# Mamba-2 scan outputs: running sums spread by one product of ones with rows at their own partitions, and a new order of VectorE's boundary work

## The chip, the cores and the metric

One core of one Trainium2 chip runs the whole program in one launch. The metric is the device time in microseconds (us) of an execution; the median of three runs before the change is 5008.08 us.

## The reference

The model is a two-layer backbone over 512 latent tokens and 256 context tokens of width 1024. Each layer has a token mixer (a pooling branch beside a bidirectional Mamba-2 scan) and a product-key expert retrieval. The change lies in the scan's outputs alone. There, tokens are cut into chunks ("tiles" below) of 128, and for each chunk, direction and head:

```python
a_cum = jnp.cumsum(dtc * a, axis=2)                     # running sums in a chunk of 128 tokens
seg = a_cum[:, :, :, None] - a_cum[:, :, None, :]
decay = jnp.exp(jnp.where(lower, seg, -jnp.inf))
cb = jnp.einsum("bclgn,bcsgn->bclsg", cc, bc)
wgt = cb[..., None] * decay * dtc[:, :, None]
y = jnp.einsum("bclsgr,bcsgrp->bclgrp", wgt, xc)        # inside the chunk
y = y + jnp.einsum("bclgn,bcgrpn->bclgrp", cc, h_in) * jnp.exp(a_cum)[..., None]   # from the state
```

Then `d_skip * x` is added to y and the sum is multiplied by `silu(z)`, with a mean square over each of four groups of channels. There are 16 heads in 4 groups of 4, and two directions.

## The kernel before, in words

`stage_outputs` computes this. It runs three times: once for the context of layer 0 (2 tiles), once for the latents of layer 0 and once for those of layer 1 (4 tiles each). Each call is a block of its own: all engines meet before it and after it. No DMA is issued inside it.

A tile (t) has 8 **units**: two directions d times four groups g, called u0 to u7 below (u0 to u3 are d = 0). For each unit:

- GpSimd (POOL) copies the 4 heads' step decays, each repeated along 128 columns, into one of four buffers `dtab` (L855).
- TensorE (PE) multiplies those with a triangle of ones, one 128x128 product for each head (L890): this gives the running sum of every token spread over all partitions, in one of three PSUM banks (`SUMS`). The signal is `acum_ready`.
- ScalarE (ACT) takes the difference to the token's own running sum with four Relu (L929, one for each head) and one Exp (L933) into one of four buffers `m_buf`.
- VectorE (DVE) multiplies with the masked C·B product `cbm` (L966). The signal is `m_ready`.
- PE multiplies the result with dt·x (L872, "intra") and adds it up in the two Y banks. It does so with a lag of two units (`LAG = 2`): in its slot of unit n, PE runs the L890 products of unit n and then the L872 products of unit n-2.

Work that comes once or twice in a tile (**boundary work**):

- PE: C·B for the tile (L883) ahead of u0's products; the product with the incoming state (L902, `inter`), once for each direction, in the slots of u2 and u6, both into the same two banks `INT`, after DVE has read the one before (`inter_read`).
- DVE: two masks of C·B (L958) at u0; `add_y(t-1)` (L945) before u1's product, which reads the Y banks of the tile before and so lets PE start the L872 of the new tile (`y_read`, waited for at u0's L872); `gate(t-1)` (L951) and the skip term (L973) after u1's; the read of `INT` (L978) and its sum (L982) after u3's and u7's.
- ACT: four squares of the tile before (L914) after u3.
- POOL: dt·x of the next tile (L847, two products over 1024 columns) behind the `dtab` copy of u4; it waits for `y_ready` of the tile before.

Every engine goes through its list in program order, and all waits are on semaphores. The order is written by hand.

Of the kernel before, what the change touches and what calls it, by code (L numbers as in the profile page):

```python
# [29 lines left out]
ALU = mybir.AluOpType  # L30
# [4 lines left out]
P = 128  # L35
# [6 lines left out]
HEADS, HEAD_DIM, GROUPS = 16, 64, 4  # L42
HPG = HEADS // GROUPS
# [59 lines left out]
def setup(nc, ctx, io):  # L103
    k = Bag()
# [116 lines left out]
     k.dots, k.lhs_ready, k.slot_free, k.acc_ready, k.acc_read, k.copy_proj, k.copy_ready) = k.sig.values()  # L221
    k.stored = Signal(k, "stored")
    k.decay_ready = Signal(k, "decay_ready")
    for name in ("turn", "h", "proj", "evac", "pad", "conv", "out"):
        k.pre[name] = Signal(k, "pre_" + name)
    k.pre_kept = [Signal(k, f"pre_kept{i}") for i in range(4)]
# [19 lines left out]
def bc(ap, shape):  # L246

    return ap.unsqueeze(2).to_broadcast(shape)
# [565 lines left out]
def stage_outputs(k, stream):  # L814

    nc = k.nc
    T = SEQ if stream == 0 else CTX_LEN
    NT = T // P
# [1 line left out]
    v = mixer_views(k)  # L820
    s = v.scr
    cbm = s[:, 0:1024].rearrange("p (d c) -> p d c", d=2)
    dtab = s[:, 1024:3072].rearrange("p (a h c) -> p a h c", a=4, h=HPG)
    m_buf = s[:, 3072:5120].rearrange("p (a h c) -> p a h c", a=4, h=HPG)
    xd = k.arena[:, A_HT:A_HT + 4 * D].rearrange("p (a d c) -> p a d c", a=2, d=2)
    ysum = s[:, 5120:5120 + D]
# [12 lines left out]
    with nc.Block() as block:  # L839
        @block.gpsimd  # L840
        def _(pool):
            def scale_x(t):

                if t >= 2:
                    pool.wait_ge(k.y_ready.sem, k.y_ready.at(t - 1))
                for dd in range(2):
                    pool.tensor_tensor(heads(xd[:, t % 2, dd]), heads(v.xtok[:, t]),  # L847
                                       bc(v.dt[:, t, dd * 16:dd * 16 + 16], [P, HEADS, HEAD_DIM]), ALU.mult) \
                        .then_inc(k.xd_ready.sem, 1)

            for n, (t, d, g) in enumerate(units):
                if n >= 4:
                    pool.wait_ge(k.acum_ready.sem, k.acum_ready.at(n - 3))
                h0 = d * 16 + g * HPG
                pool.tensor_copy(dtab[:, n % 4], bc(v.dta[:, t, h0:h0 + HPG], [P, HPG, P])) \  # L855
                    .then_inc(k.dtab_ready.sem, 1)
                if n == 0:
                    scale_x(0)
                if g == 0 and d == 1 and t + 1 < NT:
                    scale_x(t + 1)  # L860

        @block.tensor
        def _(pe):
            def intra(n):
                t, d, g = units[n]
                pe.wait_ge(k.m_ready.sem, k.m_ready.at(n + 1))
                pe.wait_ge(k.xd_ready.sem, k.xd_ready.at(2 * t + 2))
                if d == 0 and g == 0 and t >= 1:
                    pe.wait_ge(k.y_read.sem, k.y_read.at(t))
                for h in range(HPG):  # L870
                    hh = g * HPG + h
                    last = nc.tensor.matmul(k.ps[:, Y + g // 2, (hh % 8) * HEAD_DIM:(hh % 8 + 1) * HEAD_DIM],  # L872
                                            m_buf[:, n % 4, h], xd[:, t % 2, d, hh * HEAD_DIM:(hh + 1) * HEAD_DIM],
                                            start=(d == 0 and hh % 8 == 0), stop=(d == 1 and hh % 8 == 7),
                                            skip_group_check=True)
                last.then_inc(k.y_ready.sem if g == GROUPS - 1 and d == 1 else k.group_summed.sem, 1)

            for n, (t, d, g) in enumerate(units):
                if d == 0 and g == 0:
                    if t >= 1:  # L880
                        pe.wait_ge(k.cb_masked.sem, k.cb_masked.at(t))
                    for gg in range(GROUPS):
                        last = nc.tensor.matmul(k.ps[:, CB, gg * P:(gg + 1) * P], v.BT[:, gg, t * P:(t + 1) * P],  # L883
                                                v.CT[:, gg, t * P:(t + 1) * P], start=True, stop=True)
                    last.then_inc(k.cb_ready.sem, 1)
                pe.wait_ge(k.dtab_ready.sem, k.dtab_ready.at(n + 1))
                if n >= 3:
                    pe.wait_ge(k.seg_ready.sem, k.seg_ready.at(n - 2))
                for h in range(HPG):
                    last = nc.tensor.matmul(k.ps[:, SUMS[n % 3], h * P:(h + 1) * P], dtab[:, n % 4, h], k.tri[:, d],  # L890
                                            start=True, stop=True)
                last.then_inc(k.acum_ready.sem, 1)
                if n >= LAG:
                    intra(n - LAG)
                if g == 2 and (t, d) in inters:
                    i = inters.index((t, d))
                    if i >= 1:
                        pe.wait_ge(k.inter_read.sem, k.inter_read.at(i))
                    o = order(d, t)
                    h_in = k.hfin[:, d] if o == 0 else v.hin[:, d, o - 1]  # L900
                    for gg in range(GROUPS):
                        last = nc.tensor.matmul(k.ps[:, INT + gg // 2, (gg % 2) * GW:(gg % 2 + 1) * GW],  # L902
                                                v.CT[:, gg, t * P:(t + 1) * P], h_in[:, gg * GW:(gg + 1) * GW],
                                                start=True, stop=True)
                    last.then_inc(k.inter_ready.sem, 1)
            for n in range(len(units) - LAG, len(units)):
                intra(n)

        @block.scalar
        def _(act):  # L910
            def squares(t):
                act.wait_ge(k.gated.sem, k.gated.at(t + 1))
                for g in range(GROUPS):
                    nc.scalar.activation(sq, v.zs[:, t, g * GW:(g + 1) * GW], ACT.Square,  # L914
                                         accum_out=ss[:, t, g:g + 1])
                    act.drain()

            for n, (t, d, g) in enumerate(units):
                act.wait_ge(k.acum_ready.sem, k.acum_ready.at(n + 1))
                if n >= 4:  # L920
                    tt, dd, gg = units[n - 4]
                    if (dd, gg) == (1, GROUPS - 1):
                        act.wait_ge(k.y_ready.sem, k.y_ready.at(tt + 1))
                    else:
                        act.wait_ge(k.group_summed.sem, k.group_summed.at(n - 3 - tt))
                for h in range(HPG):
                    col = d * 16 + g * HPG + h

                    last = nc.scalar.activation(m_buf[:, n % 4, h], k.ps[:, SUMS[n % 3], h * P:(h + 1) * P], ACT.Relu,  # L929
                                                bias=v.cum[:, t, col:col + 1], scale=-1.0)  # L930
                last.then_inc(k.seg_ready.sem, 1)
                act.drain()
                nc.scalar.activation(m_buf[:, n % 4], m_buf[:, n % 4], ACT.Exp, scale=-1.0) \  # L933
                    .then_inc(k.decay_ready.sem, 1)
                if (d, g) == (0, 3) and t >= 1:
                    squares(t - 1)
            squares(NT - 1)

# [1 line left out]
        def _(dve):  # L940
            def add_y(t):
# [3 lines left out]
                nc.vector.tensor_tensor(ysum, ysum, k.ps[:, Y:Y + 2].rearrange("p a b -> p (a b)"), ALU.add) \  # L945
                    .then_inc(k.y_read.sem, 1)

            def gate(t):

                dve.drain()  # L950
                nc.vector.tensor_tensor(v.zs[:, t], v.zs[:, t], ysum, ALU.mult).then_inc(k.gated.sem, 1)  # L951

            for n, (t, d, g) in enumerate(units):
                if d == 0 and g == 0:
                    dve.wait_ge(k.cb_ready.sem, k.cb_ready.at(t + 1))
                    cb = k.ps[:, CB].rearrange("p (g c) -> p g c", g=GROUPS)
                    for dd in range(2):
                        last = nc.vector.tensor_tensor(cbm[:, dd].rearrange("p (g c) -> p g c", g=GROUPS), cb,  # L958
# [1 line left out]
                                                       ALU.mult)  # L960
                    last.then_inc(k.cb_masked.sem, 1)
                    dve.drain()
                if g == LAG - 1 and d == 0 and t >= 1:
# [5 lines left out]
                if g == LAG - 1 and d == 0:  # L969
                    if t >= 1:  # L970
                        gate(t - 1)
                        dve.drain()
                    nc.vector.tensor_tensor(heads(ysum), heads(v.xtok[:, t]),  # L973
                                            bc(v.hrow[:, HR_SKIP:HR_SKIP + 16], [P, HEADS, HEAD_DIM]), ALU.mult)
                if g == 3 and (t, d) in inters:
                    i = inters.index((t, d))
                    dve.wait_ge(k.inter_ready.sem, k.inter_ready.at(i + 1))
                    nc.vector.tensor_tensor(heads(ytmp), heads(k.ps[:, INT:INT + 2].rearrange("p a b -> p (a b)")),  # L978
                                            bc(v.eac[:, t, d * 16:d * 16 + 16], [P, HEADS, HEAD_DIM]), ALU.mult) \
                        .then_inc(k.inter_read.sem, 1)  # L980
                    dve.drain()
                    nc.vector.tensor_tensor(ysum, ysum, ytmp, ALU.add)  # L982
            add_y(NT - 1)
            gate(NT - 1)
    n = len(units)
# [2 lines left out]
    for x in (k.y_ready, k.y_read, k.gated, k.cb_ready, k.cb_masked):  # L988
        x.advance(NT)
    k.group_summed.advance(n - NT)  # L990
    k.xd_ready.advance(2 * NT)
    for x in (k.inter_ready, k.inter_read):
        x.advance(len(inters))
# [1491 lines left out]
```

## Time and profile before

| what | us |
|---|---|
| runs, median of 3 | 5008.08 (5007.76 to 5017.28) |
| the profiled execution, its own time | 5002.69 |
| its span, first to last instruction | 5000.9 |
| mean granted clock of PE | 0.844 |
| scan outputs, context of layer 0 | 227.8 to 284.0: 56.2 |
| scan outputs, latents of layer 0 | 1396.9 to 1508.7: 111.8 |
| scan outputs, latents of layer 1 | 3276.1 to 3386.2: 110.1 |

The three stages make 278.1 us, 5.6% of the span. The times of the stages are the windows between the first instruction of a stage and the first of the next one. Inside them a tile is read best off ACT: each unit starts with a group of four L929, so the starts of those groups are the beats of the stage, and an idle time printed behind one tells what ACT waited for.

### The profile page before, as it was taken

What the parts mean: (1) busy time and instruction counts of PE and PEld (TensorE: products, weight loads), DVE (VectorE), ACT (ScalarE), POOL (GpSimd) and SP (SyncE); (2) the same over time, 40 slices, a digit from 0 to 9 for tenths busy, and PEclk for the clock granted to TensorE, in tenths of its full rate; (3) what the DMA queues carried; (4) which work ended last, traced back from release to release, by engine and by line L of the source; (5) the groups of instructions that cost most, each with busy time, mean ns of one, the idle gap of its engine ahead of it and who ended that gap; (6) DMA issues with size and microseconds to landing.
All of it is one profiled execution on the core that took longest, in us unless ns stands there. A gap on an engine that the chain in (4) does not pass through costs nothing. (4 is left out here: it accounts for less than half of the span.)

```text
span 5000.9 us, 49209 instructions
## 1 busy us (share of the span) xinstructions
PE 3547.0 (71%) x15992; PEld 1834.1 (37%) x15992; DVE 3231.2 (65%) x6604; ACT 1513.1 (30%) x3714; POOL 2222.5 (44%) x1683
## 2 busy tenths in 40 slices
PE   7888888997578987555555557979988555555555
PEld 5677424332277434111111115877843111111111
DVE  5255687664465567676776766466457777777775
ACT  2352344343142224322222223243222222222221
POOL 3253444443033354555555552333335555555553
PEclk8889999999788998777777778889999777777777
DMA  5436999998603799999999992102279999999998
GB/s 181 177 106 226 376 422 400 419 426 368 259 1 114 278 421 397 413 415 422 403 425 412 414 421 81 68 1 93 77 273 405 423 414 420 419 416 420 414 415 369
DMA packets 251729, 1575.63 MB, mean 315 GB/s; under 512 B 42560, under 2 KB 49216, under 8 KB 65472
## 3 DMA queue, kind: packets, MB, share of 16 engines
q0 software_dynamic: 184320, 1342.26, 64.8%
q1 hardware_dynamic: 67152, 230.23, 12.5%
q8 instruction: 127, 2.08, 0.2%
q14 instruction: 130, 1.06, 0.1%
HBM read 1554.88 MB, written 17.50 MB: 314 GB/s over the span
## 5 line engine op out<-in xcount | busy, mean ns | idle before, releaser
L2349 PE MATMUL banks<-arena 128*64 128x512 f32 x5120 | 1591.6, 759 | 1107.8 <-ACT arena L2177 1107.1
L1964 POOL DMA_INDIRECT arena<-in_experts,arena x1280 | 1504.7, 1176 | 1635.1 <-PE banks L2349 1375.2
L2050 DVE CUSTOM_DVE_ANT_0 arena<-arena,token_copies 128x1024 f32<-128x1024 f32 x1280 | 1636.1, 1297 | 674.1 <-DMA arena<-in_experts,arena 611.6
L2349 PEld LDWEIGHTS banks<-arena 128*64 128x64 f32 x5120 | 385.5, 166 | 2150.6 <-ACT arena L2177 1526.0
L2170 ACT ACTIVATE arena<-arena 128x2 f32<-128x2 f32 x640 | 131.2, 205 | 1797.6 <-DVE arena L2050 1797.1
L282 POOL TENSOR_TENSOR wide_low<-wide_blocks,wide_high 128x1024 fp32r<-128x1024 f32 x136 | 342.8, 2542 | 554.1 <-ACT wide_high L272 554.1
L2177 ACT ACTIVATE arena<-arena 128x64 f32<-128x64 f32 x1280 | 376.2, 340 | 285.2 <-POOL arena L1835 244.3
L2233 PE MATMUL banks<-arena,wide_blocks 128*128 128x512 f32 (+3 forms) x960 | 310.7, 473 | 8.6 <-ACT arena L2079 6.7
L320 PE MATMUL banks<-activation_a,wide_high 128*128 128x512 f32 (+1 forms) x768 | 278.5, 363 | 8.5 <-ACT arena L344 2.7
L2301 PE MATMUL banks<-arena,wide_blocks 128*128 128x512 f32 x576 | 276.2, 617 | 0.0
L322 PE MATMUL banks<-activation_a,wide_low 128*128 128x512 f32 (+1 forms) x768 | 269.5, 351 | 0.0
L855 POOL COPY arena<-arena 128x512 f32<-128x512 f32 x80 | 63.2, 802 | 415.7 <-SPq L839 306.4
L2233 PEld LDWEIGHTS banks<-arena,wide_blocks 128*128 128x128 f32 x960 | 164.5, 202 | 132.3 <-issue 113.5
L321 PE MATMUL banks<-activation_b,wide_high 128*128 128x512 f32 (+1 forms) x512 | 180.1, 352 | 0.0
L2170 ACT ACT_TABLE_LOAD x134 | 171.9, 1283 | 4.7 <-issue 0.4
L1793 POOL TENSOR_TENSOR arena<-arena 128x512 f32<-128x512 f32 x80 | 111.2, 1390 | 136.6 <-DVE arena L1774 135.1
L272 ACT CAST wide_high<-wide_blocks 128x1024 fp32r<-128x1024 f32 x136 | 135.4, 1046 | 103.1 <-PE banks L320 45.6
L2301 PEld LDWEIGHTS banks<-arena,wide_blocks 128*128 128x128 f32 x576 | 104.1, 193 | 164.2 <-issue 162.2
L320 PEld LDWEIGHTS banks<-activation_a,wide_high 128*128 128x128 f32 x768 | 151.3, 197 | 30.8 <-ACT arena L344 3.5
L1835 POOL TENSOR_TENSOR arena<-fold,arena 128x1024 f32<-128x1024 f32 x80 | 161.3, 2017 | 1.5
L322 PEld LDWEIGHTS banks<-activation_a,wide_low 128*128 128x128 f32 x768 | 150.7, 196 | 19.0
L672 DVE SCALAR_TENSOR_TENSOR arena<-arena 128x256 f32<-128x256 f32 (+1 forms) x128 | 138.8, 1085 | 10.3 <-issue 0.9
(252 smaller groups left out, 4969.6 us busy)
## 6 DMA issues: line engine op xcount, KB each, us to landing
wide_blocks<-in_wide SPq DMA_DIRECT2D x168, 1024.0 KB, 4.9
arena<-in_experts,arena POOLq DMA_INDIRECT x1280, 10.6
pre_scan<-arena SPq DMA_DIRECT2D x16, 256.0 KB, 7.3
arena<-pre_scan SPq DMA_DIRECT2D x16, 256.0 KB, 5.5
residual<-in_tokens SPq DMA_DIRECT2D x6, 512.0 KB, 7.5
arena<-mod_rows SPq DMA_DIRECT2D x6, 512.0 KB, 7.7
norm_rows<-in_keys SPq DMA_DIRECT2D x3, 1024.0 KB, 5.0
pre_z<-arena SPq DMA_DIRECT2D x8, 256.0 KB, 7.5
```

Source lines behind the costliest of these rows:

```text
L282: k.nc.gpsimd.tensor_tensor(k.wide_lo[:, n % WIDE_SLOTS, rows], k.wide[:, n % WIDE_SLOTS, rows], k.wide_hi[:, n % HI_SLOTS, rows].bitcast( ...
L320: signal_used(k, nc.tensor.matmul(out, lh, rh, start=(kt == 0), stop=False))
L321: nc.tensor.matmul(out, lh, rl, start=False, stop=False)
L322: last = nc.tensor.matmul(out, ll, rh, start=False, stop=(kt == KT - 1))
L1835: nc.gpsimd.tensor_tensor(masks, k.fold[:].unsqueeze(1).to_broadcast(shape), bc(gate[:, u % 2].rearrange("p s j -> p (s j)"), shape), ALU. ...
L1964: pool.indirect_dma_start(out=v.ring[:, g % RING], out_offset=None, in_=io["experts"], in_offset=bass.IndirectOffsetOnAxis(ap=c.idx[:, u % ...
L2050: last = nc.vector.tensor_tensor_reduce(out=u_row, in0=u_row, in1=k.copies[:, n % NJ], scale=1.0, scalar=0.0, op0=ALU.mult, op1=ALU.add, a ...
L2170: nc.scalar.activation(c.gel[:, a:a + NJ], c.act_in[:, a:a + NJ], ACT.Gelu_apprx_tanh)
L2177: last = nc.scalar.activation(v.lhs[:, g % 4, j], c.masked[:, q * NJ + j], ACT.Copy, scale=c.gel[:, a + j:a + j + 1])
L2233: last = nc.tensor.matmul(k.ps[:, 2 + i % 2, cut], k.wide[:, n % WIDE_SLOTS, kt, (m % 2) * P:(m % 2 + 1) * P], v.h2T[:, kt, cut], start=(k ...
L2301: last = nc.tensor.matmul(k.ps[:, 5 + e % 2, 0:AT], w[:, kt, (e - 1) % 2 * P:((e - 1) % 2 + 1) * P], v.hT[:, kt], start=(kt == 0), stop=(k ...
L2349: mm = nc.tensor.matmul(k.ps[j * QUAD:(j + 1) * QUAD, a + half], v.lhs[:, g % 4, j], v.ring[:, (g * NJ + j) % RING, D + half * BANK:D + (h ...
```

## The change

The running sums exist already: `v.cum`, tokens on partitions, 32 columns for 2 x 16 heads. The new kernel transposes them once at the start of the stage (PE, one transpose for each tile, into the `INT` banks), ACT copies them to `cum_rows` (32 partitions, one for each direction and head), and for each unit POOL multiplies them with four columns of the identity matrix into `spread` (32 partitions, 4 x 128 columns, three buffers instead of four). One product of ones (32 x 128) with these 512 columns, a single matmul in the program, puts each head's sums on all partitions. Then the order of the boundary work changes: C·B of the next tile goes into the slot of u5, `inter` of d = 0 into the slot of u3 (d = 1 stays in u6), ACT's squares behind u5; on DVE the read and sum of `INT` for d = 1 go behind u2 of the **next** tile (for the last tile they stay behind u7), the gate behind u3, the skip term behind u4, the read and sum for d = 0 behind u5.

```diff
-    dtab = s[:, 1024:3072].rearrange("p (a h c) -> p a h c", a=4, h=HPG)
+    spread = s[0:32, 1024:2560].rearrange("p (a h c) -> p a h c", a=3, h=HPG)
+    cum_rows = s[0:32, 2560:2560 + T].rearrange("p (t c) -> p t c", t=NT)
@@ POOL
-                if n >= 4:
-                    pool.wait_ge(k.acum_ready.sem, k.acum_ready.at(n - 3))
+                if n == 0:
+                    pool.wait_ge(k.cum_moved.sem, k.cum_moved.at(1))
+                if n >= 3:
+                    pool.wait_ge(k.acum_ready.sem, k.acum_ready.at(n - 2))
-                pool.tensor_copy(dtab[:, n % 4], bc(v.dta[:, t, h0:h0 + HPG], [P, HPG, P])) \
+                pool.tensor_tensor(spread[:, n % 3], bc(k.ident[0:32, h0:h0 + HPG], [32, HPG, P]),
+                                   cum_rows[:, t].unsqueeze(1).to_broadcast([32, HPG, P]), ALU.mult) \
@@ PE
+            def both(t):
+                if t >= 1:
+                    pe.wait_ge(k.cb_masked.sem, k.cb_masked.at(t))
+                for gg in range(GROUPS):
+                    last = nc.tensor.matmul(k.ps[:, CB, gg * P:(gg + 1) * P], v.BT[:, gg, t * P:(t + 1) * P],
+                                            v.CT[:, gg, t * P:(t + 1) * P], start=True, stop=True)
+                last.then_inc(k.cb_ready.sem, 1)
+            for t in range(NT):
+                last = nc.tensor.transpose(k.ps[0:32, INT, t * P:(t + 1) * P], v.cum[:, t, 0:32], k.ident[:])
+            last.then_inc(k.cum_turned.sem, 1)
+            both(0)
             for n, (t, d, g) in enumerate(units):
-                if d == 0 and g == 0: [C·B of tile t]
+                if d == 1 and g == 1 and t + 1 < NT:
+                    both(t + 1)
-                for h in range(HPG):
-                    last = nc.tensor.matmul(k.ps[:, SUMS[n % 3], h * P:(h + 1) * P], dtab[:, n % 4, h], k.tri[:, d],
-                                            start=True, stop=True)
+                nc.tensor.matmul(k.ps[:, SUMS[n % 3]], k.ones[0:32], spread[:, n % 3].rearrange("p h c -> p (h c)"),
+                                 start=True, stop=True).then_inc(k.acum_ready.sem, 1)
-                if g == 2 and (t, d) in inters:
+                if g == 3 - d and (t, d) in inters:
@@ ACT
+            act.wait_ge(k.cum_turned.sem, k.cum_turned.at(1))
+            nc.scalar.copy(cum_rows.rearrange("p t c -> p (t c)"), k.ps[0:32, INT, 0:T]).then_inc(k.cum_moved.sem, 1)
-                if (d, g) == (0, 3) and t >= 1:
+                if (d, g) == (1, 1) and t >= 1:
                     squares(t - 1)
@@ DVE
+            def add_inter(t, d):    [L978 and L982 as before, with a drain ahead]
+                if (d, g) == (0, 1) and t >= 1:    add_y(t - 1), then u1's product
+                if (d, g) == (0, 2) and t >= 1:    add_inter(t - 1, 1)
+                if (d, g) == (0, 3) and t >= 1:    gate(t - 1)
+                if (d, g) == (1, 0):               the skip term
+                if (d, g) == (1, 1):               add_inter(t, 0)
+                if (t, d, g) == (NT - 1, 1, 3):    add_inter(t, 1)
```

The lines under "DVE" are shortened: each names the condition and what follows the unit's product under it. A drain is added ahead of the two masks L958.

## Rows read from the trace of the kernel before

**Rows 1.** Windows: start:end, length, busy of each engine, PE clock, DMA, GB/s.
```profile
1422.98:1449.39 26.41, 21.95 (x155) 20.67 (x153) 16.98 (x18) 15.76 (x49) 10.46 (x10) 0.87 0.00 1
...
1476.22:1500.30 24.08, 19.83 (x144) 18.54 (x142) 14.58 (x16) 15.75 (x48) 2.85 (x4) 0.93 0.00 1
...
3301.29:3326.56 25.27, 20.81 (x155) 19.64 (x153) 16.97 (x18) 15.76 (x48) 10.46 (x10) 0.93 0.01 1
3326.56:3353.75 27.19, 22.45 (x155) 21.17 (x153) 16.98 (x18) 15.76 (x48) 10.46 (x10) 0.87 0.00 1
...
251.81:276.16 24.35, 19.66 (x136) 18.46 (x134) 14.58 (x16) 15.64 (x48) 2.85 (x4) 0.86 0.00 1
```
**Rows 2.** Timeline at a tile's start (u0 at 3326.56): start, length, engine, line [idle before].
```profile
3328.35 1.14 ACT L929 ACTIVATE arena<-banks,arena 128x128 f32<-128x128 f32 x4
3328.83 1.28 DVE L958 TENSOR_TENSOR arena<-banks,triangles 128x512 f32<-128x512 f32 x2
3329.24 4.21 POOL L847 TENSOR_TENSOR arena<-arena 128x1024 f32<-128x1024 f32 x2 [2.03 <-PE banks L872]
3330.21 1.48 DVE L966 TENSOR_TENSOR arena<-arena 128x512 f32<-128x512 f32 x1
3331.78 1.22 DVE L945 TENSOR_TENSOR arena<-arena,banks 128x1024 f32<-128x1024 f32 x1
...
3333.15 1.94 PE L872 MATMUL banks<-arena 128*128 128x64 f32 x8 [3.05 <-DVE arena L945]
...
3334.88 3.73 PE L902 MATMUL banks<-arena 128*128 128x256 f32 x8
...
3340.24 1.14 ACT L929 ACTIVATE arena<-banks,arena 128x128 f32<-128x128 f32 x4 [8.25 <-PE banks L890]
...
3344.34 1.14 ACT L929 ACTIVATE arena<-banks,arena 128x128 f32<-128x128 f32 x4
```
**Rows 3.** Timeline: units whose DVE product lands late, without and with `inter` behind it.
```profile
236.78 2.34 DVE L966 TENSOR_TENSOR arena<-arena 128x512 f32<-128x512 f32 x1 [2.40 <-ACT arena L933]
240.12 1.11 PE L890 MATMUL banks<-triangles,arena 128*128 128x128 f32 x8
241.27 1.15 ACT L929 ACTIVATE arena<-banks,arena 128x128 f32<-128x128 f32 x4 [0.65 <-PE banks L890]
...
3319.32 0.69 DVE L966 TENSOR_TENSOR arena<-arena 128x512 f32<-128x512 f32 x1 [0.57 <-ACT arena L933]
3320.07 1.10 PE L872 MATMUL banks<-arena 128*128 128x64 f32 x8 [1.42 <-DVE arena L966]
3323.88 1.14 ACT L929 ACTIVATE arena<-banks,arena 128x128 f32<-128x128 f32 x4 [1.11 <-PE banks L890]
```
**Rows 4.** Timeline: PE idle of 2.68 us and what follows; four 512-column records of another stage.
```profile
1482.43 1.33 PE L872 MATMUL banks<-arena 128*128 128x64 f32 x8 [2.68 <-DVE arena L945]
1483.55 3.41 PE L902 MATMUL banks<-arena 128*128 128x256 f32 x8
...
1101.74 1.98 PE L2301 MATMUL banks<-arena,wide_blocks 128*128 128x512 f32 x4
```
**Rows 5.** Single lines (L855, L1793, L847): count, ns min/median/max, first and last start.
```profile
L855 POOL COPY arena<-arena x80: 599/613/1607, 227.8 to 3365.4; 128x512 f32<-128x512 f32 x80
...
L1793 POOL TENSOR_TENSOR arena<-arena x80: 1261/1283/2213, 446.3 to 4906.5; 128x512 f32<-128x512 f32 x80
...
L847 POOL TENSOR_TENSOR arena<-arena x20: 1889/1896/2352, 228.4 to 3331.1; 128x1024 f32<-128x1024 f32 x20
```
**Rows 6.** Timeline: u0 of the stage at 3276.16; an ACT copy; eight transpose records; a read of `INT`.
```profile
3279.98 1.14 ACT L929 ACTIVATE arena<-banks,arena 128x128 f32<-128x128 f32 x4 [28.50 <-PE banks L890]
...
1520.76 0.69 ACT L1607 ACTIVATE activation_a<-banks,arena 128x512 fp32r<-128x512 f32 x1 [8.61 <-PE banks L1573]
...
3386.24 1.94 PE L332 MATMUL banks<-identity,residual 128*128 128x128 f32 x8 [6.52 <-PEq L839]
...
3343.13 1.21 DVE L978 TENSOR_TENSOR arena<-banks,arena 128x1024 f32<-128x1024 f32 x1
```

More of the change, by code:

```diff
@@ L223, in setup @@
     k.decay_ready = Signal(k, "decay_ready")
+    k.cum_turned = Signal(k, "cum_turned")
+    k.cum_moved = Signal(k, "cum_moved")
     for name in ("turn", "h", "proj", "evac", "pad", "conv", "out"):
@@ L876, in intra @@
                 last.then_inc(k.y_ready.sem if g == GROUPS - 1 and d == 1 else k.group_summed.sem, 1)
-            for n, (t, d, g) in enumerate(units):
[L879 to L885, printed above, removed]
+            def both(t):
[9 more added lines that the diff above has]
+            both(0)
+            for n, (t, d, g) in enumerate(units):
+                if d == 1 and g == 1 and t + 1 < NT:
+                    both(t + 1)
                 pe.wait_ge(k.dtab_ready.sem, k.dtab_ready.at(n + 1))
@@ L888, in _ @@
                     pe.wait_ge(k.seg_ready.sem, k.seg_ready.at(n - 2))
-                for h in range(HPG):
-                    last = nc.tensor.matmul(k.ps[:, SUMS[n % 3], h * P:(h + 1) * P], dtab[:, n % 4, h], k.tri[:, d],
-                                            start=True, stop=True)
-                last.then_inc(k.acum_ready.sem, 1)
+                nc.tensor.matmul(k.ps[:, SUMS[n % 3]], k.ones[0:32], spread[:, n % 3].rearrange("p h c -> p (h c)"),
+                                 start=True, stop=True).then_inc(k.acum_ready.sem, 1)
                 if n >= LAG:
                     intra(n - LAG)
-                if g == 2 and (t, d) in inters:
+                if g == 3 - d and (t, d) in inters:
                     i = inters.index((t, d))
@@ L946, in add_y, with add_inter @@
                     .then_inc(k.y_read.sem, 1)
+            def add_inter(t, d):
+                if (t, d) in inters:
+                    i = inters.index((t, d))
+                    dve.wait_ge(k.inter_ready.sem, k.inter_ready.at(i + 1))
+                    dve.drain()
+                    nc.vector.tensor_tensor(heads(ytmp), heads(k.ps[:, INT:INT + 2].rearrange("p a b -> p (a b)")),
+                                            bc(v.eac[:, t, d * 16:d * 16 + 16], [P, HEADS, HEAD_DIM]), ALU.mult) \
+                        .then_inc(k.inter_read.sem, 1)
+                    dve.drain()
+                    nc.vector.tensor_tensor(ysum, ysum, ytmp, ALU.add)
             def gate(t):
@@ L955, in _ @@
                     dve.wait_ge(k.cb_ready.sem, k.cb_ready.at(t + 1))
+                    dve.drain()
                     cb = k.ps[:, CB].rearrange("p (g c) -> p g c", g=GROUPS)
@@ L962, in _ @@
                     dve.drain()
-                if g == LAG - 1 and d == 0 and t >= 1:
+                if (d, g) == (0, 1) and t >= 1:
                     add_y(t - 1)
@@ L968, in _ @@
                                         ALU.mult).then_inc(k.m_ready.sem, 1)
[L969 to L972, printed above, removed]
+                if (d, g) == (0, 2) and t >= 1:
+                    add_inter(t - 1, 1)
+                if (d, g) == (0, 3) and t >= 1:
+                    gate(t - 1)
+                    dve.drain()
+                if (d, g) == (1, 0):
                     nc.vector.tensor_tensor(heads(ysum), heads(v.xtok[:, t]),
                                             bc(v.hrow[:, HR_SKIP:HR_SKIP + 16], [P, HEADS, HEAD_DIM]), ALU.mult)
[L975 to L982, printed above, removed]
+                if (d, g) == (1, 1):
+                    add_inter(t, 0)
+                if (t, d, g) == (NT - 1, 1, 3):
+                    add_inter(t, 1)
             add_y(NT - 1)
@@ L990, in stage_outputs @@
     k.group_summed.advance(n - NT)
+    k.cum_turned.advance(1)
+    k.cum_moved.advance(1)
     k.xd_ready.advance(2 * NT)
```

## The prediction

> **What bounds the kernel now.** I read the 40 slices of the page first: the three stages that the change touches are short (278.1 of 5000.9 us) and no DMA runs in them, so whatever they give or lose moves everything behind them rigidly; each ends in a meeting of all engines. Then the windows by tile. Tiles that are neither first nor last in their stage ("middle", four of them: 26.41, 26.83, 25.27 and 27.19 us, mean 26.43) and last tiles (24.08 twice, 24.35) have no engine that is full: in 27.19 us PE is busy 22.45, DVE 16.98, ACT 15.76, POOL 10.46 [rows 1]. So I went to the timeline of a tile's start and took ACT's beats. u1 comes 1.79 us after u0 [rows 2]; that is the beat of a unit where nothing stalls (the four Relu and the Exp make 1.77). u4 comes 4.10 us after u3, since ACT's squares lie between. The hole is between u2 and u3: ACT idles 8.25 us. Its cause is read backwards: PE idles 3.05 us until `add_y` (L945) ends at 3333.00, which is 6.44 us after u0's start; then L872, `inter` (L902) and the sums run at PE's half clock (1.94 and 3.73 us) before u3 can start at 3340.24. `add_y` is late because DVE first does the read and sum of `INT` behind u7 and the masks, and then its product of u0 takes 1.48 us. The other two idle times of a tile are 1.11 us (`inter` in u6's slot, [rows 3]) and under 1 us (C·B).
>
> **The port.** POOL's two dt·x products start at 3329.24; the first takes 1.89 us [rows 5] and ends near 3331.13; DVE's product was issued at 3330.21 and ends at 3331.69, 0.56 us after that, and POOL's pair takes 4.21 us where twice 1.89 is 3.78. So a POOL operation and a DVE operation that both read SBUF (DVE with two inputs there) go one after the other. `add_y`, with one input in PSUM, took its 1.22 us right in the middle of POOL's second product [rows 2]. This is the weight on the other pan of the change: DVE's gated work in a tile is 8 products at about 0.6 plus four sums of 1.15 (twice L982, gate, skip) = 9.4 us; POOL's is 8 x 0.61 + 3.78 = 8.7 us now. With the new product p in place of the copy it is 8p + 3.78. The Trainium skill (SBUF — State Buffer, section "Who interferes with whom") says of this port that the lock is exclusive, held for the whole instruction, and taken by VectorE operations with two SBUF inputs against GpSimd operations that read SBUF; it makes no exception for an operation on 32 partitions. By that rule the figures below stand; without it I would take 1 us off each middle tile, 4 us in all.
>
> **Part 1, the new product on POOL.** 80 copies of 0.61 us go, 80 products on 32 partitions come. No row shows one. Bounds: 0.61 us (the copy of the same 512 columns) and 1.28 us (L1793, 512 columns, two full inputs) [rows 5]. The nearest row is L847: also one input repeated along the columns, 1.89 us for 1024; half is 0.95, and a fixed part goes on top. I take p = 1.1. POOL then has 8 x 1.1 + 3.78 = 12.6 us a tile, no bound by itself; with DVE's 9.4 the port is taken for 22.0 us a middle tile. [...]
>
> **Part 2, the product on PE.** Four 128x128 products (8 records, 1.11 us [rows 3]) go, one with 512 columns comes. Its two records start 0.46 us apart and last 0.59 ((1.98 - 0.59) / 3 from four such records [rows 4]): 1.05 us. The columns are the same in number; six weight loads are gone. I take 0.06 us a unit, which shortens only ways that PE is on; it is within the rounding below. Nothing to win here either way.
>
> **Part 3, the order, in a middle tile.** Time zero is u0's start on ACT. The chain I use: a unit's DVE product starts 1.9 us after its Relu and ends at 2.6; from the end of a DVE product (or of `add_y`) to the start of the unit that its L872 holds up it is 2.15 us (236.78 + 2.34 = 239.12 to 241.27), with `inter` between 3.87 us (3320.01 to 3323.88) [rows 3]. From the end of an `INT` read to that start it is 3.87 - 0.9 (the L872) = 2.95.
> - u7's product of the tile before ends at 0.85; the masks (1.28) until 2.15; POOL's product for u4 holds the port until about 2.8; u0's product until 3.5; `add_y` until 4.7. Hence u3 at 4.7 + 2.15 = 6.85 (before: 13.68).
> - POOL's dt·x pair alternates with u1's product: 3.4 to 5.3, DVE to 5.9, 5.9 to 7.8; so u2's product ends at 8.4 instead of 6.1.
> - Now a **new wait**: `inter` of d = 0 sits in u3's slot and may write `INT` only after DVE has read the sum of the tile before, which stands behind u2's product: 8.4 + 1.3 = 9.7 (L978 is 1.21 us, [rows 6]). Queued behind it on PE are the sums of u4, and ACT behind them: u4 at 9.7 + 2.95 = 12.65, where the beat alone would give 8.6.
> - u5 has C·B before it: 2.7 (1.79 + 0.9) later, 15.35. The squares: u6 4.10 later, 19.45 (the distance from 3340.24 to 3344.34, [rows 2]).
> - The same wait again: `inter` of d = 1 needs the read of d = 0, which is behind u5's product (15.35 + 2.85 = 18.2, read at 19.45); u7 at 19.45 + 2.95 = 22.4; next u0 1.75 later: 24.15.
>
> PE idles 1.3 us before u0's L872 and about 2.05 us before the first `inter`. What is its clock then? An idle time of 1.42 us [rows 3] left it at full (L872 took 1.10), one of 2.68 us was followed by `inter` at 3.41 us, one of 3.05 by 3.73 [rows 2, 4]; at full clock `inter` adds 1.72 us (3.87 - 2.15). Mine lies between; half speed for `inter` and the sums behind it is up to 2.4 us, of which I take 0.45. So 24.6, a gain of 1.8 us, four times: **7.2 us**. Bounds: 22.0 (the port alone) and 26.4.
>
> **Last tiles.** No dt·x pair, no C·B. `add_y` ends at 4.2, u3 at 6.35; u2's product at 6.1, `INT` read 7.4, u4 10.35; u5 12.1, u6 16.2; u5's product waits for the gate, u4's product (12.95) and the skip term, ends 14.8, read 16.0, u7 18.95, its Exp ends 20.8, against 24.08: 3.3 us, twice. In the context the last tile has no `inter` for d = 1: u7 at 17.95, end 19.8 against 24.35: 4.5. Together **11.1 us**. The tail behind it (last sums, gate, squares) keeps its order and its cost.
>
> **Start and first tile.** New and on the path: four transposes at half clock, 1.94 us (8 records, [rows 6]), the ACT copy 0.69, POOL's product 1.1, the sums at half clock about 1.9: u0 at 5.7 where it was 3.82 (3279.98 - 3276.16). POOL then does its dt·x pair before u1's product, as before, so u1 is 2.8 late (1.9 plus twice 0.5). Part of it comes back, since `inter` leaves u2's slot; but in u6's slot it waits for the read behind u5. I get the second tile's u0 at 26.8 after the stage's start in the latents, where it was 25.1 and 26.0 (+1.7, +0.8), and 23.5 against 24.0 in the context (-0.5). Together **+2.0 us**; ends 0 and +7.5 (2.5 each).
>
> **Sum.** -7.2 - 11.1 + 2.0 = -16.3 us. The profiled execution took 5002.69, so 4986.4 for such a one; the median of the runs shown is 5.4 us above it, so 5008.1 - 16.3 = **4992 us**.
>
> **Rivals.**
> - *Larger gain.* POOL's product near 0.61 us and hits on the port rare: `add_y` ends at 4.1, u2's product at 6.1, its read at 7.4; u4 10.35, u5 13.0, u6 17.1, u7 20.1, next u0 21.9. Four times 4.5, last tiles 11.1, start 0: 29 us, 4979 us. For it: the port is free for much of the time in the rows of before; against it: no POOL row with two inputs is under 1.26 us.
> - *Nothing left.* The port is the bound of the middle tile: 8p + 3.78 + 9.4 reaches the old 26.4 at p = 1.65, and already at 1.28 (23.4) any miss in the turns brings it near 26. Then the middle tiles give 0, last tiles 9 (their port is freer), the start takes 5: 4 us, 5004 us.
> - *Slower.* The new waits on `INT` drop PE's clock, and it stays at 1.2 GHz. The place is u3's to u6's slots; the price: at half clock a unit costs PE 2 x 1.78 = 3.56 us instead of 1.79, which is no longer hidden behind ACT; three units and `inter` (another 1.7) make 7 us in each of 7 tiles, 49 us, against the 29 that the new order frees at best: 20 us slower, 5028 us. It decides where PE's idle time before `inter` exceeds 2.7 us and PE does not recover in the two units behind it. Against it: in the rows of before, PE was back at full speed one or two units after the hole (granted clock 0.87 to 0.93 over the tiles, [rows 1]).
> - *It does not read ahead*: the sum of a tile is read earlier only in name if DVE reaches it late; that is inside the first part of the forecast.
>
> **Chances.** Forecast 0.48, larger gain 0.22, nothing left 0.18, slower 0.12. The 8-in-10 range goes from 4972 (the larger gain with a rest) to 5008 (nothing left with the worst start); it leaves the slower case out. A measurement of this kernel tells 0.2% (10 us) from no change. Faster by more: nearly all of the first two but a tenth of the forecast, 0.64; within 0.2%: 0.22; slower: 0.14.
>
> **What would show it.** Right: ACT's hole between u2 and u3 shrinks from 8.25 us to between 1 and 2; a new one of 3 to 5 us ahead of u4, with PE's L902 waiting for DVE's read of `INT`; one of 1 to 2 ahead of u7; middle tiles near 24.6, last tiles near 21; POOL's product between 1.0 and 1.3 us where DVE isn't in its way; u0 of a stage 1.5 to 2.5 us later. Wrong: no wait of L902 (then the larger gain), DVE products of over 1.5 us in most units (the port), L902 at 3.4 us and more in most tiles (the clock).

## The result, and the profile after

| kernel | runs | median, us | ratio to before (95% interval) |
|---|---|---|---|
| before | 4 | 5007.92 | |
| changed | 4 | 5107.11 (5102.20 to 5118.71) | 1.0198 (1.018 to 1.0216), 2% slower |

The forecast was 4992 us, 16 us faster; the measured time is 99 us slower and lies outside the range. The profiled execution took 5102.20 us with a span of 5100.4, against 5002.69 and 5000.9.

First the page of the changed kernel: engines, then the granted clock of PE in 40 slices.

```profile
PE 3689.0 (72%) x15522; PEld 1849.1 (36%) x15522; DVE 3242.1 (64%) x6604; ACT 1516.5 (30%) x3717; POOL 2248.4 (44%) x1683
...
PEclk8778999998767898877777777867999777767777
```

PE is busy for 142 us more, with 470 records fewer: each takes longer. The windows of the three stages that changed say where (start:end, length, PE, PEld, DVE, ACT, POOL busy, PE clock, DMA share, GB/s), and the last line is one tile, the third of the last stage.

```profile
226.95:302.14 75.19, 66.98 (x194) 42.00 (x194) 30.79 (x30) 32.53 (x97) 25.36 (x20) 0.55 0.00 1
1416.92:1564.66 147.74, 137.27 (x420) 85.98 (x420) 68.82 (x68) 64.90 (x193) 53.17 (x40) 0.59 0.00 0
3334.87:3486.49 151.62, 142.40 (x420) 89.46 (x420) 69.67 (x68) 64.92 (x193) 52.36 (x40) 0.57 0.00 0
...
3408.55:3442.77 34.22, 34.22 (x105) 21.60 (x105) 16.57 (x17) 16.09 (x48) 13.65 (x10) 0.60 0.00 1
```

The stages took 278.0 us together before and take 374.6 now: 96.6 of the 99.5 us by which the span grew. The tile tells the rest: PE is busy in all 34.22 of 34.22 us, and the granted clock is 0.60. Before, the worst middle tile had PE busy in 22.45 of 27.19 us at 0.87 [rows 1]. So in this tile it is no wait of any kind; PE never stops, and it runs at 1.2 GHz for about four fifths of the time (0.8 x 0.5 + 0.2 x 1 = 0.60).

Rows of the timeline of that tile (L902 is the new product of ones, L878 the product with dt·x, L913 `inter`, L942 the Relu of a unit):

```profile
3414.24 2.07 PE L902 MATMUL banks<-arena,ones 32*128 32x512 f32 x2
3416.24 1.97 PE L878 MATMUL banks<-arena 128*128 128x64 f32 x8
3416.35 1.14 ACT L942 ACTIVATE arena<-banks,arena 128x128 f32<-128x128 f32 x4 [2.05 <-PE banks L902]
3416.39 1.03 POOL L860 TENSOR_TENSOR arena<-identity,arena 32x512 f32<-32x512 f32 x1 [2.87 <-PE banks L902]
3418.14 2.07 PE L902 MATMUL banks<-arena,ones 32*128 32x512 f32 x2
3420.14 1.97 PE L878 MATMUL banks<-arena 128*128 128x64 f32 x8
3420.25 1.14 ACT L942 ACTIVATE arena<-banks,arena 128x128 f32<-128x128 f32 x4 [2.05 <-PE banks L902]
...
3425.80 3.08 PE L913 MATMUL banks<-arena 128*128 128x256 f32 x8
...
3431.85 1.12 PE L902 MATMUL banks<-arena,ones 32*128 32x512 f32 x2
3432.90 1.10 PE L878 MATMUL banks<-arena 128*128 128x64 f32 x8
...
3434.99 1.97 PE L878 MATMUL banks<-arena 128*128 128x64 f32 x8
3436.95 3.78 PE L913 MATMUL banks<-arena 128*128 128x256 f32 x8
...
3440.66 2.07 PE L902 MATMUL banks<-arena,ones 32*128 32x512 f32 x2
```

A unit takes 3.90 us where the beat of before was 1.79 [rows 2]: from start to start 2.00 for L902 and 1.90 for L878, the same L878 that took 1.10 at full clock [rows 3] and takes 1.10 here at 3432.90. The full clock comes for two units in this tile, behind one `inter` (L913, 128 rows, 3425.80), and is gone again at 3434.99. Behind the other `inter` (3436.95) it does not come: the L902 after it takes 2.07 us. The guess on which the experiments were built is that the product on 32 rows keeps PE from the full clock.

POOL's new operation is where it was expected:

```profile
L860 POOL TENSOR_TENSOR arena<-identity,arena x80: 1028/1029/1527, 228.0 to 3464.2; 32x512 f32<-32x512 f32 x80
```

### The profile page after: what moved, and what is told of

It reads as the page before. It is cut to its first block and busy times, and to the rows that moved or that the text cites. A ratio compares the mean times of both kernels' runs of the same rounds, so it can differ in the third digit from the quotient of the medians.

```text
span 5100.4 us, 48300 instructions
## 1 busy us (share of the span) xinstructions
PE 3689.0 (72%) x15522; PEld 1849.1 (36%) x15522; DVE 3242.1 (64%) x6604; ACT 1516.5 (30%) x3717; POOL 2248.4 (44%) x1683
## 5 line engine op out<-in xcount | busy, mean ns | idle before, releaser
L2375 PE MATMUL banks<-arena 128*64 128x512 f32 x5120 | 1609.2, 767 | 1096.7 <-ACT arena L2203 1095.7
L860 POOL TENSOR_TENSOR arena<-identity,arena 32x512 f32<-32x512 f32 x80 | 92.1, 1156 | 481.2 <-ACT arena L930 306.5
L322 PE MATMUL banks<-activation_a,wide_high 128*128 128x512 f32 (+1 forms) x768 | 278.0, 362 | 8.5 <-ACT arena L346 2.7
L992 DVE TENSOR_TENSOR arena<-arena 128x512 f32<-128x512 f32 x80 | 71.9, 901 | 159.9 <-ACT arena L946 159.8
L878 PEld LDWEIGHTS banks<-arena 128*128 128x128 f32 x640 | 125.3, 293 | 93.3 <-issue 69.6
```

Of the source, the lines that this page charges most:

```text
L322: signal_used(k, nc.tensor.matmul(out, lh, rh, start=(kt == 0), stop=False))
L2375: mm = nc.tensor.matmul(k.ps[j * QUAD:(j + 1) * QUAD, a + half], v.lhs[:, g % 4, j], v.ring[:, (g * NJ + j) % RING, D + half * BANK:D + (h ...
```

## The experiments

Theory A: the product on 32 rows keeps PE from the full clock. Theory B: it is the number of weight loads or records (2 instead of 8). Theory C: the new order makes holes, and the holes drop the clock. All kernels below compute the whole output.

The yardstick beside the time is the sum of the three stages in the profiled execution, first instruction of the stage to the first of the next one (before: 56.2 + 111.7 + 110.0 = 278.0 us). It is free of the drift of the rest of the program, but it is one execution of each kernel; the ratios rest on all runs, and the two differ by up to 15 us (rows64: 48.6 by the stages, about 64 by the ratio). The ratios are against runs of the kernel before in the same session. There were three sessions after that of the result, on three chips, with medians of before of 5008.35 us (rows128, order_only, product_only, four_by_32), 5012.58 (rows64, rows96, pool_mult, read_early) and 5008.17 (order_late, early_late); so ratios are compared below, and medians only with care.

| kernel | time, median | against before (95%) | stages, us | middle tiles, us |
|---|---|---|---|---|
| before | 5007.92 to 5012.58 | | 278.0 | 25.27 to 27.19 |
| changed | 5107.11 | 1.0198 (1.018 to 1.0216) | 374.6 | 34.2 to 34.8 |
| product_only | 5100.87 | 1.0182 (1.0142 to 1.0222) | 362.1 | 32.7 to 35.4 |
| four_by_32 | 5101.13 | 1.0187 (1.0164 to 1.0209) | 382.4 | 32.0 to 39.4 |
| rows64 | 5069.32 | 1.0128 (1.0107 to 1.0149) | 326.6 | 27.5 to 34.2 |
| rows96 | 5032.68 | 1.0052 (1.0032 to 1.0071) | 301.2 | 27.6 to 27.8 |
| rows128 | 5021.94 | 1.0034 (1.0021 to 1.0046) | 288.1 | 25.2 to 27.0 |
| pool_mult | 5011.60 | 1.0002 (0.9989 to 1.0014) | 277.6 | 24.7 to 26.9 |
| order_only | 4992.38 | 0.9969 (0.9955 to 0.9983) | 261.1 | 23.99 |
| read_early | 4992.39 | 0.9964 (0.9951 to 0.9978) | 259.2 | 23.1 to 24.8 |
| order_late | 5005.74 | 0.9998 (0.9987 to 1.0009) | 266.9 | 25.0 to 26.6 |
| early_late | 4993.08 | 0.9961 (0.9947 to 0.9975) | 255.4 | 22.2 to 23.9 |

### rows128: the same product on 128 rows

```diff
-    spread = s[0:32, 1024:2560]...
+    wide_spread = s[0:128, 1024:2560]        # set to zero once, at the stage's start, by POOL
-    pool.tensor_tensor(spread[:, n % 3], ...
+    pool.tensor_tensor(spread[0:32, n % 3], ...
-    nc.tensor.matmul(..., k.ones[0:32], spread[:, n % 3]...)
+    nc.tensor.matmul(..., k.ones[0:128], spread[:, n % 3]...)
```

> The changed kernel, but the product of ones has 128 rows: the tile spread spans 128 partitions, of which rows 32 to 127 are set to zero once at the start of the stage. Columns, number of matmuls and weight loads, and order stay. Theory A (the 32-row product keeps PE at half clock: in the changed kernel a unit took 3.90 us with PE never idle, 2.07 for the product and 1.97 for L878): granted clock in the stages back at 0.85 and more, L902 about 1.05 us and L878 about 1.0 a unit, units at 1.8 to 2.1 us, whole 4985 to 5000 us. Theory B (it is the number of weight loads or records that counts, 2 instead of 8): no change, 5105 us. Theory C (the holes of the new order drop the clock): no change, 5105 us.

Measured: 5021.94 us, 1.0034 (1.0021 to 1.0046). Of the 96.6 us, 86.5 are gone (stages 288.1). The units are back at 1.75 us; rows of its timeline, L905 being the product of ones and L881 the one with dt·x:

```profile
1449.58 1.08 PE L905 MATMUL banks<-arena,ones 128*128 128x512 f32 x2
1450.62 1.10 PE L881 MATMUL banks<-arena 128*128 128x64 f32 x8
1451.56 1.08 PE L905 MATMUL banks<-arena,ones 128*128 128x512 f32 x2
1451.81 4.21 POOL L851 TENSOR_TENSOR arena<-arena 128x1024 f32<-128x1024 f32 x2
1452.04 2.22 DVE L995 TENSOR_TENSOR arena<-arena 128x512 f32<-128x512 f32 x1
1454.35 1.22 DVE L961 TENSOR_TENSOR arena<-arena,banks 128x1024 f32<-128x1024 f32 x1
1455.72 1.66 PE L881 MATMUL banks<-arena 128*128 128x64 f32 x8 [3.08 <-DVE arena L961]
1457.17 2.02 PE L905 MATMUL banks<-arena,ones 128*128 128x512 f32 x2
```

The added rows are zeros, so what counts is the rows that the matmul spans, not the numbers in them. Theory A's clock is right; its time was not: I expected 4985 to 5000 and got 5022. The rows show where part of the remainder lies: POOL's pair (L851) takes the port 0.23 us ahead of DVE's product of u0, that product takes 2.22 us, `add_y` (L961) is late, and PE idles 3.08 us and comes back at half clock, just as before the change.

### product_only, four_by_32, rows64, rows96

product_only is the kernel before with nothing but the new product (transposes, ACT copy, POOL's product, one 32-row matmul) in the old order. four_by_32 is the changed kernel with the matmul cut in four:

```diff
-    nc.tensor.matmul(k.ps[:, SUMS[n % 3]], k.ones[0:32], spread[:, n % 3]..., ...)
+    for h in range(HPG):
+        last = nc.tensor.matmul(k.ps[:, SUMS[n % 3], h * P:(h + 1) * P], k.ones[0:32], spread[:, n % 3, h], ...)
```

> The old order with the new product of 32 rows. Theory A: half clock in most units, 3.9 us a unit, whole 5090 to 5125 us. Theory C: about 5010 us, within 10 us of before.

> The changed kernel, but the 32-row product of 512 columns is cut into four of 128 columns: 8 records and 8 weight loads a unit as before the change, still 32 rows. Theory A (rows): still half clock, 5100 us or a few more. Theory B (weight loads): full clock, 4985 to 5000 us.

Both came out as theory A had it: 1.0182 and 1.0187. Theory B falls with the second (8 weight loads, 8 records, still slow) and with rows128 (2 records, units at 1.75 us), theory C with the first (old order, still slow). A window of 60 us in each, product_only first, then four_by_32:

```profile
1460.00:1520.00 60.00, 60.00 (x171) 37.74 (x172) 31.23 (x28) 26.68 (x81) 24.33 (x17) 0.57 0.00 1
```
```profile
1460.00:1520.00 60.00, 60.00 (x270) 52.10 (x270) 30.27 (x30) 28.04 (x85) 24.86 (x18) 0.61 0.00 1
```

PE is busy for 60 of 60 us in both, at 0.57 and 0.61.

rows64 and rows96 are rows128 with `wide_spread = s[0:64, ...]` and `s[0:96, ...]`.

> The changed kernel with 64 rows in the product of ones (rows 32 to 63 are zeros), else as rows128. Theory A as a matter of degree: between 5101 (32 rows) and 5022 us (128 rows), around 5060 to 5090, with part of the units at 3.9 us. Theory A as a switch between 32 and 64 rows (for example because 32 rows are one of four row groups): like rows128, 5015 to 5030 us. If what helped rows128 was the memset ahead of the stage and not the rows, this is at 5022 as well.

> The same with 96 rows. By degree: 5020 to 5050 us, between rows64 and rows128. By a switch between 32 and 64 rows: 5015 to 5030 us as rows128.

1.0128 and 1.0052: over whole stages it is a matter of degree, 374.6, 326.6, 301.2 and 288.1 us with 32, 64, 96 and 128 rows. Between 96 and 128 rows the step is shown by the stages of single executions alone; the intervals of the times overlap (1.0032 to 1.0071 and 1.0021 to 1.0046). With 64 rows the two stages of the latents differ: middle tiles of 27.7 and 27.5 us in one and of 34.2 and 34.2 in the other. The same code fell on either side. The two slow tiles have the memset in front of their stage and still take what they took in the changed kernel, so the memset is not what helped.

### order_only: the other half of the change

The old sums (`dtab`, four products with the triangles) in the new order.

> The new order of the boundary work with the old sums (POOL copies into four buffers of dtab, four 128x128 products with the triangles, no transposes, no ACT copy). Theory A (32 rows): clock as before the change, ACT's hole ahead of u3 shrinks, middle tiles 23 to 25 us instead of 26.4, whole 4975 to 4992 us. Theory C (order drops the clock): about 5100 us.

Measured 4992.38 us, 0.9969 (0.9955 to 0.9983): 0.4 us above the upper edge of what was expected, and a gain that a measurement can tell from none. The middle tiles, two of the four, and the start of one (L951 `add_y`, L960 the read of `INT`, L908 `inter`, L985 DVE's product, L849 POOL's pair):

```profile
1411.17:1435.16 23.99, 19.30 (x155) 18.45 (x154) 17.95 (x18) 15.91 (x49) 10.94 (x11) 1.00 0.00 1
1435.16:1459.15 23.99, 19.30 (x155) 18.45 (x154) 17.94 (x18) 15.91 (x49) 10.93 (x11) 1.00 0.00 1
```
```profile
1413.62 0.69 DVE L985 TENSOR_TENSOR arena<-arena 128x512 f32<-128x512 f32 x1
1413.64 4.75 POOL L849 TENSOR_TENSOR arena<-arena 128x1024 f32<-128x1024 f32 x2 [2.03 <-PE banks L874]
...
1415.55 3.38 DVE L985 TENSOR_TENSOR arena<-arena 128x512 f32<-128x512 f32 x2
...
1415.78 1.08 PE L874 MATMUL banks<-arena 128*128 128x64 f32 x8 [1.27 <-DVE arena L951]
...
1417.84 1.14 ACT L935 ACTIVATE arena<-banks,arena 128x128 f32<-128x128 f32 x4 [1.44 <-PE banks L896]
...
1419.03 1.23 DVE L960 TENSOR_TENSOR arena<-banks,arena 128x1024 f32<-128x1024 f32 x1
...
1420.31 1.99 PE L908 MATMUL banks<-arena 128*128 128x256 f32 x8 [1.67 <-DVE arena L960]
...
1423.23 1.14 ACT L935 ACTIVATE arena<-banks,arena 128x128 f32<-128x128 f32 x4 [3.54 <-PE banks L896]
```

These answer to [rows 2]: ACT's idle time ahead of u3 went from 8.25 to 1.44 us, and a new one of 3.54 stands ahead of u4, with PE waiting 1.67 us for the read of `INT`. PE's idle times of 1.27 and 1.67 left its clock at full (1.00 over the tile).

### pool_mult: what POOL's longer operation costs by itself

```diff
-    pool.tensor_copy(dtab[:, n % 4], bc(v.dta[...], [P, HPG, P]))
+    pool.tensor_tensor(dtab[:, n % 4], bc(v.dta[...], [P, HPG, P]), k.ones[:].unsqueeze(1).to_broadcast([P, HPG, P]), ALU.mult)
```

> order_only, but POOL makes dtab by a product with ones (two SBUF inputs, 1.03 us expected) instead of a copy (0.61 us); results, PE's work and order stay. Theory P (the 30 us between order_only, 4992, and rows128, 5022, is the port that POOL's longer operation takes from DVE): 5008 to 5022 us, DVE's u0 product late, middle tiles 26 instead of 23.99. Theory S (it is the start chain and PE's form, two records instead of eight): under 4998 us, middle tiles under 24.5.

Measured 5011.60 us, 1.0002 (0.9989 to 1.0014), stages 277.6: 0.4 us more for each of 80 operations eat the whole 16.9 us that the order frees. The rows are those of rows128's hole again (L986 the product of u0, L952 `add_y`):

```profile
1423.57 4.21 POOL L849 TENSOR_TENSOR arena<-arena 128x1024 f32<-128x1024 f32 x2 [1.79 <-PE banks L875]
1423.80 2.22 DVE L986 TENSOR_TENSOR arena<-arena 128x512 f32<-128x512 f32 x1
1426.11 1.22 DVE L952 TENSOR_TENSOR arena<-arena,banks 128x1024 f32<-128x1024 f32 x1
1427.48 1.08 PE L875 MATMUL banks<-arena 128*128 128x64 f32 x8 [3.04 <-DVE arena L952]
```

### read_early, order_late, early_late: the new wait, and POOL's pair

read_early is order_only with the read of `INT` for d = 1 right behind `add_y` (the sum stays behind u2):

```diff
 if (d, g) == (0, 1) and t >= 1:
     add_y(t - 1)
+    read_inter(t - 1, 1)
```

> order_only, but DVE reads INT of the tile before right behind add_y, ahead of u1's product; the sum into ysum stays behind u2. Theory W (the new wait of inter in u3's slot is what u3 to u4 costs, 5.39 us): u3 to u4 goes from 5.39 to 3.4 or so in middle tiles, u1's product is 1.3 us later and hits nothing; middle tiles 21.8 to 22.4, last tiles 0 to 1 shorter, whole 4980 to 4987 us (order_only 4992). Rival: u1's product, now late, holds inter's slot just as long: no change, 4989 to 4995 us.

0.9964 (0.9951 to 0.9978), not told apart from order_only's 0.9969. The wait is real, but smaller than I priced: u3 to u4 went from 5.39 to 4.52 us in all four middle tiles (expected 3.4), because u1's product, now behind the read, met POOL's pair at the port. The median of 4992.39 us lies in the range of the rival (4989 to 4995), and the middle tiles took 23.1 to 24.8 us where 21.8 to 22.4 was expected. In two of the four tiles, u6 to u7 took 4.83 instead of 3.16 us. What happens there is told at early_late.

order_late and early_late move POOL's pair from u4 to u6 (`if g == 2 and d == 1`), the first on order_only, the second on read_early.

> order_only, but POOL's dt.x pair for the next tile goes behind the copy of u6 instead of u4, that is about two units later, away from add_y and the products of u0 to u2. Theory Q (the port at the tile's start is what still delays DVE there: u1's and u2's products together took 3.38 us): u3 to u4 from 5.39 to 3.6 in middle tiles, middle tiles from 23.99 to 22.2 to 22.8, whole 4984 to 4989 us. Rival: the pair only moves its contention to the gate and the skip term, and PE idles as long elsewhere: 4990 to 4996 us.

> read_early with the same move of POOL's pair. With Q: u3 to u4 at 3.0 to 3.5 us, middle tiles 21.7 to 22.3, whole 4980 to 4986 us. Rival as in order_late: 4988 to 4994 us.

order_late lost nearly all of the order's gain by the time, 0.9998 (0.9987 to 1.0009), and 5.8 of 16.9 us by the stages (266.9 against 261.1); the median of 5005.74 us is above both ranges. The pair didn't leave the tile's start; it came later into it, right onto u1's and u2's products, and the read of `INT` behind u2 paid (L849 the pair, L985 the products, L908 `inter`, L896 the sums):

```profile
1422.55 4.21 POOL L849 TENSOR_TENSOR arena<-arena 128x1024 f32<-128x1024 f32 x2
1422.95 4.36 DVE L985 TENSOR_TENSOR arena<-arena 128x512 f32<-128x512 f32 x2
...
1428.67 2.72 PE L908 MATMUL banks<-arena 128*128 128x256 f32 x8 [2.52 <-DVE arena L960]
...
1431.19 1.92 PE L896 MATMUL banks<-triangles,arena 128*128 128x128 f32 x8
```

Behind this idle time of 2.52 us `inter` took 2.72, 3.63 and 2.98 us in three of the four middle tiles, that is at half clock for a part of it, and 1.99 us in the fourth. POOL runs up to four units ahead, and "behind u6" on its list is u2's time on the others': I had placed it by its own list. early_late, where the read is no longer behind u2, came near what was expected at u3 to u4 (3.63 us, expected 3.0 to 3.5) and had the shortest stages of all (255.4), but in three of four middle tiles u6 to u7 took 4.5 to 4.8 us:

```profile
1449.51 3.20 PE L908 MATMUL banks<-arena 128*128 128x256 f32 x8 [1.75 <-DVE arena L966]
1452.51 1.56 PE L896 MATMUL banks<-triangles,arena 128*128 128x128 f32 x8
1454.10 1.14 ACT L935 ACTIVATE arena<-banks,arena 128x128 f32<-128x128 f32 x4 [2.97 <-PE banks L896]
```

There PE's idle time of 1.75 us was followed by `inter` at 3.20 us. In the latents' stages of early_late the same 1.75 us was followed by 2.56 to 3.21 us four times and by 1.99 twice; in order_only by 1.99 five times and by 3.30 once. So times of this length fall on either side. The time, 4993.08 us, lies in the rival's range, and 0.9961 (0.9947 to 0.9975) is not told apart from order_only or read_early. Any of these three beats both kernels, by 0.3 to 0.4% against before.

## Why the prediction was wrong

**The step that failed is Part 2**, "Nothing to win here either way": the columns are the same in number, so I costed the product on PE at nothing. The 1.05 us that I took for it is right at full clock (1.12 in the changed kernel, 1.08 on 128 rows), and nearly a factor of two off in 55 of the 80 units, where it took 1.91 to 2.07 us. It matters twice, since L878 beside it slows down as well: such a unit takes 3.90 us instead of 1.79. By the stages of one execution each the change divides so:

| step | stages, us | difference |
|---|---|---|
| before | 278.0 | |
| new order (order_only) | 261.1 | -16.9 |
| POOL's operation 1.03 instead of 0.61 us (pool_mult) | 277.6 | +16.5 |
| the rest of the new product at 128 rows: start chain, memset, its form (rows128) | 288.1 | +10.5 |
| 32 rows instead of 128, no memset | 374.6 | +86.5 |

The time says the same of the last step: 1.0198 against 1.0034, 1.6% or 82 us.

The clock had a place in my rivals, and the slower one named it, but with the wrong cause and a fifth of the price: it hung on PE's idle time before `inter` ("It decides where PE's idle time before `inter` exceeds 2.7 us") and gave 5028 us. In two of the four middle tiles of the changed kernel PE had no idle time at all, in the others 0.14 and 0.43 us. I had read the clock only off what followed idle times. That was enough for the rows of these stages, where every L890 and L872 spans 128 rows. But the trace of before has a stretch elsewhere that shows the other case, a product L593 of 128 rows with 32 moving columns:

```profile
3168.20:3191.60 23.40, 23.40 (x129) 23.40 (x130) 11.20 (x11) 4.47 (x6) 5.26 (x2) 0.60 0.14 47
```

PE is busy for 23.40 of 23.40 us, and the granted clock is 0.60. So a PE that never stops and yet runs mostly at the lower level stood there to be read before the change was made. It would have told me that a full PE is no proof of a full clock, though not that 32 rows do the same.

**The sum would have failed at full clock too.** rows128 keeps the whole change and gives PE its clock back, and it still takes 1.0034 of before, 5022 us, above the range. Against before, off ACT's beats:

| term | forecast, us | order_only | pool_mult | rows128 |
|---|---|---|---|---|
| start and first tiles | +2.0 | +2.3 | +6.5 | +15.2 |
| middle tiles | -7.2 | -9.7 | -3.5 | -0.6 |
| last tiles, u0 to u7 | -11.1 | -10.7 | -4.6 | -4.9 |
| together | -16.3 | -18.1 | -1.5 | +9.6 |

The sum fits order_only, which has nothing of Parts 1 and 2, and fits it in part by luck: the +2.0 counts u0 as 1.9 us late in each stage, while in order_only u0 is 0 to 0.3 us earlier than before and the first tiles add 2.3 us all the same. What the new product costs beside the clock was priced too low in every term.

**Part 3, the order, was right**, and order_only shows it almost beat by beat. Starts after u0 in a middle tile:

| | u3 | u4 | u5 | u6 | u7 | next u0 |
|---|---|---|---|---|---|---|
| forecast | 6.85 | 12.65 | 15.35 | 19.45 | 22.4 | 24.15 |
| order_only | 6.87 | 12.26 | 14.94 | 19.05 | 22.21 | 23.99 |

The new wait on `INT` stood where it was put (u3 to u4 5.39 us against 5.80), the two shorter PE idle times too. But part of the agreement is luck: the forecast was for p = 1.1, order_only has the copy of 0.61. With 1.03 (pool_mult) the middle tiles took 25.56 on average and not 24.6.

**Part 1, POOL's product, was right in size** (1.03 us, forecast 1.1) **and wrong in what it costs**. I let DVE have its product of u0 before POOL's pair. In order_only that held, but by 0.01 to 0.02 us in each of the four middle tiles (1413.62 and 1413.64 in the rows above), so this too was luck. With the longer operation POOL starts its pair 0.23 us earlier than DVE's product in pool_mult's rows; the product takes 2.22 us instead of 0.69, PE idles 3.04 us, and its clock falls. The 0.45 us for the clock was too little where this happens. The Trainium skill's rule of the exclusive port (SBUF — State Buffer, "Who interferes with whom") also holds for it: in pool_mult's rows `add_y`, with one input in PSUM, keeps its 1.22 us in the middle of the pair. For the operation itself the Trainium skill (GPSIMD Engine Reference, section 3.1) counts about 2.6 cycles an element with two inputs; at the 1.2 GHz of its example that is an estimate of 1.11 us for 512 columns, a little above the trace's 1.03. Two of my readings were off as well. DVE's work at the port is 8 products of 0.69 and four sums of 1.22, 10.4 us and not 9.4. And L1793, my upper bound, does not have two full inputs: one of them is repeated there too, over blocks of columns.

**Last tiles and start.** Last tiles of the latents took 19.11 us from u0 to u7 in order_only (forecast 18.95; before 22.2), so the order was priced right there. With POOL's longer operation they took 21.1 (pool_mult) and 21.0 (rows128), and more than half of the gain is gone. The first tiles were wrong: tile 0 of the three stages, u0 to the next u0, took 67.3 us in order_only and 77.1 in rows128, against 64.4 before. u0 itself was only 0.5 to 1.4 us late in the changed kernel, forecast 1.9; I had read the eight records of [rows 6] as four transposes, and they are eight: L893 leaves 10 records for the 10 tiles, 0.60 us for four.

**The range** left out the slower case, and with it would have ended at 5028 us, still far below 5107.

## What to carry to other kernels

In this kernel a matmul with 32 rows cost the same as one with 128 only at the same clock (1.12 and 1.08 us). Next to other work on a PE that is nearly full, ask what the clock will do, and look in the trace for stretches where PE is busy all the time and the granted clock is low all the same. If a product has 32 rows to offer, it is worth trying to pad it with zero rows to 128: here this took 86.5 of 96.6 us back, and still left the kernel slower than before. When two engines share a port, a longer operation on the one is paid where the other has its tightest chain, and moving work on an engine that runs ahead must be planned by the time at which it will run, not by its place in the list.

## What the runs showed of the hardware that I had not expected

- PE was busy 34.22 of 34.22 us, with the granted clock at 0.60, that is mostly at the lower level, while its work alternated between a product on 32 rows and one on 128. With 64, 96 and 128 rows of the same product (the added ones zero) the stages take 326.6, 301.2 and 288.1 us instead of 374.6. Eight records and weight loads a unit instead of two made no difference (four_by_32, 0.61). The Trainium skill (TensorE: Matmul & The Clock Gate, section "Why this matters for your kernels") says that a single matmul with K = 32 takes the same time as one with K = 128; L902 agrees at full clock (1.12 us against 1.08 for the product on 128 rows), but in the kernel a unit with it takes 3.90 us instead of 1.75. The same section of the Trainium skill also has it that keeping the engine continuously busy brings the fast state; no idle time, and mostly half speed, is what this trace has, and the measurement decides.
- The rows are not the only thing that matters: in the kernel before, L593, with 128 rows but only 32 moving columns, kept PE busy for 23.40 of 23.40 us at a granted clock of 0.60.
- What it is in the array that the clock answers to can't be told from these runs: they vary the rows alone, of the weights and of the moving data together, and the added rows of the moving data are zeros.
- In the latents' stages an idle time of PE of 1.75 us was followed by an `inter` at full clock (1.99 us) five times in order_only and twice in early_late, and by a slower one (2.56 to 3.30 us) once and four times. In order_only 1.27 and 1.67 us were followed by full clock; 2.52 us (order_late) by a fall in three middle tiles of four; 3.04 (pool_mult) and 3.08 us (rows128) by a fall in the rows shown.
